# Hybrid short-conv / HGRN2 trunk on one core: the keys' low part behind the second level step, and the last head's fifth output part between its last two levels

## What is computed

```
q, fpre, inp, z = jnp.split(h @ w_in, 4, axis=-1)
q = silu(q) * HEAD_DK ** -0.5
log_f = maximum(logaddexp(log(lb), log1p(-lb) + log_sigmoid(fpre)), -20)
k = -expm1(log_f)
# S_t = diag(f_t) S_{t-1} + k_t^T v_t,   o_t = q_t S_t
o = rms_norm(o, g_onorm)
y = (o * silu(z)) @ w_out          # o of all 8 heads side by side
x = x + rms_norm(y, norm_post)
```

## Time and profile before

| what | value |
|---|---|
| median of 3 runs | 1129.93 us (1129.73 to 1131.06) |
| profiled execution | 1130.89 us, its span 1129.1 us |
| TensorE busy | 1098.1 us, 97% of the span |
| VectorE, ScalarE busy | 734.8 us (65%), 374.8 us (33%) |
| mean granted TensorE clock | 0.987 of full |

### The profile page before, as it was taken

The page is one execution under the profiler, slowest core; times in us unless marked ns, Lnnn a source line. Parts: engine busy times, 40 slices in busy tenths (PEclk is TensorE's granted clock), DMA queues, the critical chain, the costliest instruction groups (busy, mean ns, idle before and its releaser), DMA issues.

```text
span 1129.1 us, 19777 instructions
## 1 busy us (share of the span) xinstructions
PE 1098.1 (97%) x7689; PEld 1038.0 (92%) x7689; DVE 734.8 (65%) x1301; ACT 374.8 (33%) x706; POOL 28.8 (3%) x36
## 2 busy tenths in 40 slices
PE   5989999999999999999999999999999999998998
PEld 4989999999999888799999999999999999987885
DVE  6697677677678547627576585765759476485246
ACT  6343333333335334432141322413223241432223
POOL 2000000000000000000001010100101001010000
PEclk7989999999999999999999999999999999999999
DMA  6102121121121533121111221211111120212053
GB/s 214 37 20 75 39 57 56 37 74 37 39 73 56 176 125 113 42 80 38 57 49 30 59 56 37 58 45 31 56 56 41 54 58 26 70 57 75 23 185 121
DMA packets 93315, 74.28 MB, mean 66 GB/s; under 512 B 2519, under 2 KB 85528, under 8 KB 93274
## 3 DMA queue, kind: packets, MB, share of 16 engines
q1 hardware_dynamic: 75482, 64.80, 18.5%
q10 hardware_dynamic: 17792, 8.91, 2.7%
HBM read 60.26 MB, written 13.44 MB: 65 GB/s over the span
## 4 chain that ended last, share of the span: by engine, by line
PE 94%; DVE 3%; DMA 1%; issue 1%; ACT 0%; SPq 0%; DVEq 0%
PE bank L546 33%; PE bank L586 25%; PE bank L682 16%; PE bank L755 4%; PE bank L566 3%; PE bank L750 1%; PE bank L803 1%; PE bank L785 1%; PE bank L835 1%; PE bank L828 1%; PE bank L837 1%; PE bank L697 1%; PE bank L663 1%; PE bank L659 1%; PE bank L763 1%
## 5 line engine op out<-in xcount | busy, mean ns | idle before, releaser
L546 PE MATMUL bank<-reg_a,wsplit 128*128 128x352 f32 x2304 | 389.9, 326 | 0.6 <-ACT arena L1183 0.6
L546 PEld LDWEIGHTS bank<-reg_a,wsplit 128*128 128x128 f32 x2304 | 368.3, 188 | 4.4 <-issue 2.3
L586 PE MATMUL bank<-reg_a,wsplit 128*128 128x264 f32 x1344 | 165.5, 284 | 1.0 <-DVE o_raw L1529 1.0
L586 PEld LDWEIGHTS bank<-reg_a,wsplit 128*128 128x128 f32 x1344 | 164.1, 188 | 1.2 <-issue 1.2
L586 PE MATMUL bank<-reg_b,w_ring 128*128 128x264 f32 x1008 | 124.7, 284 | 1.3 <-DVE wraw L1485 1.3
L586 PEld LDWEIGHTS bank<-reg_b,w_ring 128*128 128x128 f32 x1008 | 123.3, 188 | 1.5 <-DVE wraw L1485 1.5
L682 PE MATMUL bank<-reg_a,reg_b 128*128 128x512 f32 x288 | 71.1, 402 | 0.7 <-DVE reg_a L1365 0.7
L682 PE MATMUL bank<-reg_b,reg_a 128*128 128x512 f32 x288 | 68.7, 396 | 0.0
L682 PEld LDWEIGHTS bank<-reg_a,reg_b 128*128 128x128 f32 x288 | 55.1, 192 | 14.1 <-DVE reg_a L1365 0.9
L682 PEld LDWEIGHTS bank<-reg_b,reg_a 128*128 128x128 f32 x288 | 53.9, 188 | 12.5
L1736 DVE TENSOR_TENSOR arena<-arena,r_tt 128x512 f32<-128x512 f32 x40 | 27.6, 691 | 52.0 <-PE bank L755 48.5
(11 more groups left out here) (243 smaller groups left out, 1515.0 us busy)
## 6 DMA issues: line engine op xcount, KB each, us to landing
wraw<-in_w_in SPq DMA_DIRECT2D x64, 512.0 KB, 4.1
arena<-in_x_prompt SPq DMA_DIRECT2D x16, 512.0 KB, 3.7
wraw<-in_w_out SPq DMA_DIRECT2D x16, 512.0 KB, 3.3
x_scratch<-arena SPq DMA_DIRECT2D x8, 512.0 KB, 2.6
arena<-in_state_hgrn ACTq DMA_DIRECT2D x8, 512.0 KB, 3.8
out<-arena ACTq DMA_DIRECT2D x8, 512.0 KB, 2.9
arena<-x_scratch SPq DMA_DIRECT2D x8, 512.0 KB, 3.2
out<-arena SPq DMA_DIRECT2D x7, 512.0 KB, 2.6
```

Of the source, the lines that this page charges most:

```text
L546: mm = nc.tensor.matmul(bank[b][:, 0:CH], w[wi][:, k, :], rhs[hi], start=(k == 0 and i == 0), stop=(k == KT - 1 and i == 2))
L586: mm = nc.tensor.matmul(bank[banks[q]][:, 0:QT], w[wi][:, k, :], B_OP[name][hi][:, k, q * QT:(q + 1) * QT], start=(start and k == 0 and i ...
```

## The change

Three edits. In every head VectorE makes the keys' low part behind `level(h, 4)` instead of ahead of it, and TensorE waits for it behind `level(h, 8)`, just ahead of the sample products, whose own-block product comes last instead of first. In the last head the part with weight tile 4 moves from behind level 64 to between levels 32 and 64. And there `turn_lo` of the seventh head moves from behind step 5 to behind step 7.

```diff
@@ VectorE's event names
-  "qb", "k3c", "kl", "w4", "c4", "u4", "w8", ...
+  "qb", "k3c", "w4", "c4", "u4", "kl", "w8", ...
@@ TensorE, rec, s == 5
+                    pe.wait_ge(VR.sem, VR.at(h, "w4"))
+                    level(h, 8)
                     pe.wait_ge(AR.sem, AR.at(h, "kts"))
                     pe.wait_ge(VR.sem, VR.at(h, "kl"))
                     pe.wait_ge(s0_in, h * 16 + 16)
-                    pe.wait_ge(VR.sem, VR.at(h, "w4"))
-                    level(h, 8)
-                    nc.tensor.matmul(bank[7][0:NSAMP, 0:P], r_as[0:NSAMP, :], r_vt[0:NSAMP, CK * P:],
-                                     start=True, stop=False)
                     for b in range(NB):
-                        mm = nc.tensor.matmul(..., r_qb[...], r_s[:, tokens(b)], start=False, stop=(b == NB - 1))
+                        nc.tensor.matmul(..., r_qb[...], r_s[:, tokens(b)], start=(b == 0), stop=False)
+                    mm = nc.tensor.matmul(..., r_as[0:NSAMP, :], r_vt[0:NSAMP, CK * P:], start=False, stop=True)
@@ TensorE, last head
-            FILL = {3: (0,), 4: (1,), 5: (2,), 6: (3,), 7: (4,), 8: (5, 6)}
+            FILL = {3: (0,), 4: (1,), 5: (2,), 6: (3,), MID: (4,), 8: (5, 6)}
@@
                 if s == 7:
                     rec(KT - 1, MID, KT - 2)
+                    first_parts(*FILL[MID])
                 rec(KT - 1, s, KT - 2)
@@ VectorE, rec
                 elif 4 <= s <= 6:
+                    level(h, 1 << (s - 2))
                     if s == 4:
                         dve.wait_ge(AR.sem, AR.at(h, "kts"))
                         ...
-                    level(h, 1 << (s - 2))
@@ VectorE, last head
-                if s == 5:
+                if s == 7:
                     turn_lo(KT - 2)
```

More of the change, by code:

```diff
@@ L281, in build @@
         VR = Events(sem("rec_dve"), ["lb", "v3", "qc", "k", "fa", "f", "tt", "g3", "rr", "i1", "it", "i2", "q0", "q2", "q3", "k0", "k2", "k3",
-                                     "vl", "vs", "am", "as", "w2", "u2", "qb", "k3c", "kl", "w4", "c4", "u4", "w8", "c8", "u8", "w16", "c16", "u16", "w32", "c32", "u32", "ss",
+                                     "vl", "vs", "am", "as", "w2", "u2", "qb", "k3c", "w4", "c4", "u4", "kl", "w8", "c8", "u8", "w16", "c16", "u16", "w32", "c32", "u32", "ss",
                                      "sn0", "snew", "w64", "c64", "u64"]
@@ L797, in rec @@
                     pe.wait_ge(s0_in, h * 16 + 16)
-                    pe.wait_ge(VR.sem, VR.at(h, "w4"))
-                    level(h, 8)
-                    nc.tensor.matmul(bank[7][0:NSAMP, 0:P], r_as[0:NSAMP, :], r_vt[0:NSAMP, CK * P:],
-                                     start=True, stop=False)
                     for b in range(NB):
-                        mm = nc.tensor.matmul(bank[7][0:NSAMP, 0:P], r_qb[:, b * NSAMP:(b + 1) * NSAMP], r_s[:, tokens(b)],
-                                              start=False, stop=(b == NB - 1))
+                        nc.tensor.matmul(bank[7][0:NSAMP, 0:P], r_qb[:, b * NSAMP:(b + 1) * NSAMP], r_s[:, tokens(b)],
+                                         start=(b == 0), stop=False)
+                    mm = nc.tensor.matmul(bank[7][0:NSAMP, 0:P], r_as[0:NSAMP, :], r_vt[0:NSAMP, CK * P:],
+                                          start=False, stop=True)
                     mm.then_inc(PR.now("os"), 1)
```

## The result

The changed kernel takes 1131.93 us (median of 12 runs, 1131.11 to 1134.04), the kernel before 1129.74 (12 runs, 1127.93 to 1131.06). The ratio of the two is 1.0023 with a 95% interval of 1.0015 to 1.0030 (the two medians alone give 1.0019). So the change makes the kernel slower, by 2.2 us by the medians and 2.6 by the ratio, clear of no change. It lies on the border of 0.2% that the prediction named: the median is 0.3 us under 1132.2, the ratio above 1.002, and the interval reaches over both sides. The profiled execution of the changed kernel took 1134.04 us with a span of 1132.3.

The account below looks back on a forecast made before the run. TensorE's line bounds the kernel, but VectorE sets the pace from level 32 on in the last head. Terms of 0 plus the 1.24 us delay with its clock cost gave +2.32, taken as +2.5: 1132.4 us, range 1130.3 to 1134.0.

Parts of the forecast that it names:

- the border of 0.2%: Whole kernel: a measurement tells 2.26 us from no change, so 1132.2 us divides same from slower.
- Tile 4's part: Last head, between levels 32 and 64: gain 0; the wait moves before the turned keys, 2.7 us.
- The low part: Seventh head's, now ahead of tile 5's low part: the eighteen products start 1.24 us later.
- The clock: TensorE's half clock around the last head's eighteen products; three cases: 0.62 later, 2.32 later or 0.43 sooner.
- Case (b): Eighteen products: half clock lasts one more stretch, to 1036.0; they end 2.32 us later; the case taken.
- (a): Eighteen products: half clock ends at 1032.6 as before, 0.62 us later; within a rival of +0.6 to +1.3, chance 0.30.
- the length of one more stretch: Half clock around the eighteen products lasting on from 1032.6 to 1036.0, after the nearest row at 22.20 to 29.0.
- Case (c): Eighteen products: no half clock, ending 0.43 us sooner; rival forecast 1129.5 us, no difference, chance 0.08.
- The keys' edit: Keys' low part behind level 4 in every head: gain 0; rival that it held each head, -4.4 us, chance 0.04.
- the order of the products: Sample products, own-block last: 0 taken, bounds -1.6 to +1.6 us over 8 heads; rival of +1.6, chance 0.06.
- the 0.2 added for the median: Whole kernel: +2.5 taken, a little over the +2.32 sum, in case the median run lacked part of a low stretch.
- The range of 1130.3 to 1134.0: Whole kernel, in us: leaves out the -4.4 rival, about half of the no-half-clock rival and the sample-order rival's ends.

Follow-up runs that it names:

- Experiment 1: Kernel before with only the seventh head's low part moved behind step 7; 1130.82 us against 1128.75, ratio 1.0017.
- experiment 5: Changed kernel with the seventh head's low part one place later, behind tile 5's low part; ratio 1.0003 to the kernel before.
- Experiment 6: Changed kernel with 22 and 15 unread transposes filling TensorE's pauses before the turned keys and tile 5; ratio 1.0003 to the kernel before.
- 10: Experiment 9 with unread transposes in TensorE's pauses before level 4 and around the turned keys; 1125.59 us, ratio 0.9967 to the kernel before.
- 11: Kernel before with unread transposes in its four TensorE pauses; 1127.58 us, ratio 0.9984.
- experiment 9: Changed kernel, seventh head's low part back behind step 5, VectorE's sample-state scaling earlier, level-32 copies later, tile 5's low part earlier; 1127.51 us, ratio 0.9987.
- experiment 4: Kernel before with the keys' edit alone, including the new order of sample products; ratio 1.0002.

## Why the prediction was right

*Tile 4's part.* Right as it stood: level 64 at once behind the nine products, no gain, and 2.7 us before the turned keys (2.73 measured).

*The low part.* Right: 1.24 us named, 1.17 measured between the two pauses (1.88 - 0.71). Experiment 1 has all of the stretch's loss in this line, experiment 5 has it in the place and not the lateness. Tile 7's copy (1034.65, less 0.99, against 1033.75 named) and the moves (1037.01, less 0.99, against 1036.1) came as named, covered by TensorE's own delay.

*The clock.* Case (b) happened: half clock on to 1037.0 in the profiled execution, 2.20 us against the 2.32 of the sum. Experiment 6 measures the clock's part: 2.5 us in the changed kernel against 2.75 in the working. The size of that term was a little off, and for a plain reason: the prediction took a us at half clock as half a us lost, so that 4.12 us remained at full clock, and experiment 6 shows 4.28. Against these 4.28 the loss is 1.51 for 3.34 us at half clock before, and 2.53 for 5.57 in the changed kernel, 0.45 a us in both.

That it was (b) and not (a) is in part luck. The length of one more stretch was taken from one place at the start of the kernel. The mean clocks speak for more half clock in all 12 runs of the changed kernel; but in experiment 1, with the same pause before the eighteen products, only 6 of 12 are so low, and experiment 5 had the long stretch without that pause. Why the half clock lasted stays open.

Case (c), which stood on the rule of the Trainium skill ("TensorE: Matmul & The Clock Gate", section "HAM oscillation — how this bites in real kernels", place the work without gaps), did not happen. The traces agree with the rule where the gaps were filled (experiments 6, 10 and 11, granted clock 1.00 around the turned keys); this change is no such placing, since it joins some work and widens the pauses behind it. In experiment 9 the clock stayed at 1.00 there with the gaps left, so gaps do not bring half clock each time.

*The keys' edit and the order of the products.* Right at 0 each; experiment 4.

*The size.* +2.5 forecast, +2.2 measured by the medians and +2.6 by the ratio, so whether the last step, the 0.2 added for the median, was right can't be told. One execution can hide such a difference: the profiled pair differs by 3.15 us, of which 0.99 lay before the last head.

The range of 1130.3 to 1134.0 rested on what the clock might do. That stays the open part. Of the ten profiled executions with unfilled pauses around the turned keys, nine had half clock there or just behind, and that of experiment 9 had none; of the three with filled ones none had it. Which execution will have it where, and for how long, the traces do not say.

## What to carry to other kernels

When two engines hand work back and forth, find out which of them has no idle rows in the stretch; only its line counts, and filling the other's pause just moves the pause. Before putting work "into slack", look one instruction further: the same 1.25 us were free behind step 5, free again one place further back, and 1.2 us plus clock in between. And a pause of TensorE has a second price in the clock of what follows it; if it can't be closed, products that nobody reads are a cheap way not to pay that. They give back only what the clock had cost, and nothing where it had stayed up (experiment 10 against 9, around the turned keys).

## What was not expected

Dead work makes the kernel faster: 37 transposes in the pauses of the kernel before take it from 1129.77 to 1127.58 us (ratio 0.9984), and 24 in experiment 9's take that kernel from 1127.51 to 1125.59. And the clock does not fall in the same place in each execution of the same code: of the profiled ones, all with unfilled pauses waited 1.5 us before level 4; the one of experiment 5 had no half clock behind it, all others had.
